# A causal depthwise convolution shared by VectorE and GpSimd, moved wholly to VectorE

## What is computed

```
z = rms_norm(x) @ w_in                     # columns: q | k | v | a (512) | b (512)
u = a * sigmoid(b)                         # gated linear unit (GLU), 512 channels
o = band_attention(rms_norm(q), rms_norm(k), v)
c[t] = b_dw + sum_{j=0..30} w_dw[j] * u_ext[t + j]    # per channel; 30 earlier rows in front
c = silu(layer_norm(c)) @ w_pw + b_pw
x = x + concat(rms_norm(o), rms_norm(c)) @ w_out
x = x + mixture_of_experts(x);  y = x + per_layer_gate(x)
```

## Time and profile before

| what | value |
|---|---|
| median of the three runs | 1662.56 us (1661.34 to 1664.23) |
| span of the profiled execution | 1662.2 us |
| TensorE busy | 1306.2 us, 79% |
| VectorE busy | 1166.7 us, 70% |
| GpSimd busy | 925.6 us, 56% |
| ScalarE busy | 694.7 us, 42% |
| mean granted TensorE clock | 0.907 of full speed |

### The profile page before, as it was taken

The page is one execution under the profiler, slowest core; times in us unless marked ns, Lnnn a source line. Parts: engine busy times, 40 slices in busy tenths (PEclk is TensorE's granted clock), DMA queues, the critical chain, the costliest instruction groups (busy, mean ns, idle before and its releaser), DMA issues.

```text
span 1662.2 us, 18411 instructions
## 1 busy us (share of the span) xinstructions
PE 1306.2 (79%) x5969; PEld 1043.3 (63%) x5969; DVE 1166.7 (70%) x1171; ACT 694.7 (42%) x833; POOL 925.6 (56%) x829
## 2 busy tenths in 40 slices
PE   1777678887755699906888888888888888886998
PEld 0666567675633588805776666766767666744776
DVE  2279969788878422294887998888888789844442
ACT  2322223333323322212665666666666666622121
POOL 1367739999951300043777777777777777730000
PEclk9998889798766799956999999999999999997999
DMA  5311010000010332122898888889999999963320
GB/s 181 109 51 31 12 57 14 24 10 4 28 51 25 127 127 76 38 102 69 291 312 320 301 307 299 303 306 311 326 317 327 318 321 326 330 219 127 123 81 32
DMA packets 122318, 279.76 MB, mean 168 GB/s; under 512 B 17537, under 2 KB 20033, under 8 KB 122269
## 3 DMA queue, kind: packets, MB, share of 16 engines
q1 hardware_dynamic: 112477, 261.28, 45.4%
q0 software_dynamic: 9792, 17.85, 2.9%
HBM read 269.85 MB, written 27.12 MB: 179 GB/s over the span
## 4 chain that ended last, share of the span: by engine, by line
PE 34%; issue 11%; DVE 8%; ACT 2%; DMA 1%; SPq 0%; DVEq 0%; POOL 0%; POOLq 0%; ACTq 0%
PE ps L407 10%; PE ps L408 10%; PE ps L409 10%; DVE ahl L388 2%; PE ps L1615 2%; DVE mem L1538 1%; PE ps L1966 1%; ACT hhl L1075 1%; PE ps L1928 1%; DMA mem<-y_rows 1%; DVE whl L388 1%; PE ps L1862 1%; PE ps L1938 0%; DVE hhl L388 0%; DMA mem<-in_g_ple 0%
## 5 line engine op out<-in xcount | busy, mean ns | idle before, releaser
L388 DVE TENSOR_TENSOR whl<-mem,whl 128x1280 fp32r<-128x1280 f32 (+1 forms) x205 | 506.8, 2503 | 27.1 <-ACT whl L1052 25.7
L388 POOL TENSOR_TENSOR whl<-mem,whl 128x768 fp32r<-128x768 f32 (+1 forms) x213 | 467.7, 2223 | 103.1 <-ACT whl L385 62.1
L407 PE MATMUL ps<-whl,ahl 128*128 128x512 f32 x1124 | 452.9, 403 | 73.5 <-DVE ahl L388 71.4
L1052 ACT ACTIVATE whl<-mem 128x2048 fp32r<-128x2048 f32 x196 | 375.9, 1919 | 178.5 <-PE ps L409 178.5
L408 PE MATMUL ps<-whl,ahl 128*128 128x512 f32 x1124 | 444.6, 396 | 0.0
L409 PE MATMUL ps<-whl,ahl 128*128 128x512 f32 x1124 | 442.8, 394 | 0.0
L407 PEld LDWEIGHTS ps<-whl,ahl 128*128 128x128 f32 x1124 | 221.5, 197 | 128.6 <-issue 71.9
L409 PEld LDWEIGHTS ps<-whl,ahl 128*128 128x128 f32 x1124 | 219.9, 196 | 45.4
L408 PEld LDWEIGHTS ps<-whl,ahl 128*128 128x128 f32 x1124 | 220.5, 196 | 42.6 <-issue 0.2
L459 DVE SCALAR_TENSOR_TENSOR mem<-mem 128x256 f32<-128x256 f32 (+1 forms) x270 | 199.5, 808 | 0.0
L668 POOL TENSOR_SCALAR mem<-mem 128x1 f32<-128x1 f32 (+1 forms) x54 | 21.5, 397 | 318.8 <-ACT mem L875 286.3
(11 more groups left out here) (234 smaller groups left out, 1415.6 us busy)
## 6 DMA issues: line engine op xcount, KB each, us to landing
mem<-in_w_e_up SPq DMA_DIRECT2D x66, 1024.0 KB, 7.5
mem<-in_w_e_down SPq DMA_DIRECT2D x66, 1024.0 KB, 6.8
mem<-in_w_e_gate SPq DMA_DIRECT2D x66, 1024.0 KB, 5.6
mem<-in_x_prompt SPq DMA_DIRECT2D x24, 512.0 KB, 3.4
mem<-y_rows SPq DMA_DIRECT2D x16, 512.0 KB, 5.6
mem<-in_w_in SPq DMA_DIRECT2D x4, 1024.0 KB, 8.7
mem<-in_w_out SPq DMA_DIRECT2D x4, 1024.0 KB, 4.9
h_rows<-mem SPq DMA_DIRECT2D x8, 512.0 KB, 2.6
```

The lines of the kernel that those rows point to most:

```text
L388: return which.tensor_tensor(out, full, hi.bitcast(F32), ALU.subtract)
L407: nc.tensor.matmul(out, act_hi, whl[:, 0, w_at], start=first, stop=False)
L1052: nc.scalar.activation(whl[:, 0, slot * CH:(slot + 1) * CH], raw[c], ACT.Copy).then_inc(s_mhi, 1)
```

## The change

The convolution is done by VectorE alone. It has three passes, each over all four channel groups: tiles 0 to 3 (512 columns), tiles 4 to 7 (512 columns), and the sample (64 columns). That makes 372 instructions, 248 of 512 columns and 124 of 64. The first pass can't begin before four tiles of `uT` are there. The table of the GLU stage now has none after tiles 0 to 3, 18 after each of tiles 4 to 7 and 20 after tile 8. Each attention step has 18 convolution instructions before `biased(t, 0)` and 14 before `qk_sums`, and what is left at t = 9 is nothing. GpSimd's taps are gone, with the semaphore `s_convs` and its waits on the engines SP, ScalarE and TensorE.

```diff
-        CONV_PARTS = ((0, 2, KC - 1), (2, 2, KC - 1), (4, 4, KC - 1))
-        CONV_OPS = sum(channels for _, _, channels in CONV_PARTS) * TAPS
-        CONV_FIRST = 2 * (KC - 1) * TAPS
+        CONV_PARTS = ((0, 4), (4, 4), (TS, 1))
+        CONV_OPS = len(CONV_PARTS) * KC * TAPS
+        CONV_FIRST = KC * TAPS
...
-            for t0, nt, channels in CONV_PARTS:
-                w, base = nt * P, t0 * P
+            for t0, nt in CONV_PARTS:
                 for j in range(TAPS):
-                    for c in range(channels):
-                        src = uT[:, c, base + j:base + j + w].rearrange("p (t n) -> p t n", n=P)
-                        acc = R[:, t0:t0 + nt, C + c * P:C + (c + 1) * P]
+                    for c in range(KC):
+                        if t0 < TS:
+                            src = uT[:, c, t0 * P + j:(t0 + nt) * P + j].rearrange("p (t n) -> p t n", n=P)
+                            acc = R[:, t0:t0 + nt, C + c * P:C + (c + 1) * P]
+                        else:
+                            src = uT[:, c, U_SAMPLE + j:U_SAMPLE + j + SAMPLE]
+                            acc = R[:, TS, C + c * P:C + c * P + SAMPLE]
...
-                            eng.wait_ge(s_conv, n - channels + 1)
+                            eng.wait_ge(s_conv, n - KC + 1)
...
-            def sample_tap(j):
...
-            def channel_tap(j, pair, where):
...
-            def conv_steps(first, last, where):
...
-                if t >= 5:
-                    conv_steps(POOL_EARLY * (t - 5), POOL_EARLY * (t - 4), early)
-            conv_steps(4 * POOL_EARLY, POOL_BEFORE, early)
...
-                conv_steps(POOL_BEFORE + POOL_PER_TILE * t, POOL_BEFORE + POOL_PER_TILE * (t + 1), late)
-            pool.sem_inc(s_convs, 1)
...
-            CONVS_BY_TILE = (0, 0, 26, 26, 26, 26, 26, 24, 18)
+            CONVS_BY_TILE = (0, 0, 0, 0, 18, 18, 18, 18, 20)
...
-                convs(6)
+                convs(18 if t < 9 else 0)
                 if t < NT:
                     biased(t, 0)
                 if t >= 1:
                     attention_out(t - 1)
-                convs(4)
+                convs(14)
```

More of the change, by code:

```diff
@@ L253, in build_step @@
         s_o = sem("attention_normed")
-        s_convs = sem("sample_conv_done")
         s_ones = sem("ones_made")
@@ L431, in build_step @@
         LOADS = NH + NKV + 2 + 1 + NG + 2
-        CONV_PARTS = ((0, 2, KC - 1), (2, 2, KC - 1), (4, 4, KC - 1))
-        CONV_OPS = sum(channels for _, _, channels in CONV_PARTS) * TAPS
-        CONV_FIRST = 2 * (KC - 1) * TAPS
-        POOL_STEPS = 5 * TAPS
-        POOL_FIRST = 2 * TAPS
+        CONV_PARTS = ((0, 4), (4, 4), (TS, 1))
+        CONV_OPS = len(CONV_PARTS) * KC * TAPS
+        CONV_FIRST = KC * TAPS
         TAPS_AT = KC * HALO + NKV * P
@@ L580, in _ @@
             sp.wait_ge(s_conv, CONV_OPS)
-            sp.wait_ge(s_convs, 2)
             for c in (2, 3):
@@ L683, in pool_chunk @@
                 mixer_lo(pool, nc.gpsimd, s_wlp, j, lo_cut(j), chunk_size(j))
-            POOL_EARLY, POOL_BEFORE, POOL_PER_TILE = 6, 36, 14
-            acc = R[:, TS, C:2 * C].rearrange("p (c n) -> p c n", c=KC)[:, :, 0:SAMPLE]
-            early, late = qT[:, C:C + 2 * P], u2[:, C // 2:C]
-            def sample_tap(j):
[L692 to L701, removed]
@@ L994, in _ @@
             act.wait_ge(s_kv, 16 * 6)
-            act.wait_ge(s_convs, 2)
             act.wait_ge(s_oe, NT)
@@ L1733, in channel_sums @@
                     pe.wait_ge(s_conv, CONV_FIRST)
-                    pe.wait_ge(s_convs, 1)
                     pe.wait_ge(s_xl, 4 * NT)
@@ L1777, in _ @@
             pe.wait_ge(s_conv, CONV_OPS)
-            pe.wait_ge(s_convs, 2)
             channel_sums(1)
```

## The result

The changed kernel takes 1667.95 us (median of 20 runs, 1665.88 to 1671.84), the kernel before 1662.46 us beside it (20 runs, 1657.92 to 1668.78). The ratio is 1.0035 with a 95% interval of 1.0026 to 1.0045: 5.5 us slower, just beyond what a measurement can tell from no change. 8 us were forecast. The profiled execution of the changed kernel has a span of 1665.1 us, 2.9 us above the 1662.2 of the profiled one before, so the two profiles show a part of the 5.5 us only.

What follows compares the result with a forecast made beforehand. VectorE and GpSimd were taken to share the attention stage's bound and slow each other. The terms -14.4 + 45.0 - 11.6 - 9.5 - 1.5 = +8.0 us, on the median of 1662.56, gave 1670.6 us, range 1658.5 to 1678.

Steps and rivals of the forecast that it cites:

- Price of an instruction: VectorE's convolution instructions without GpSimd's taps: 0.66 us for 512 columns, 0.19 for 64, in all 187 us.
- first taps: First instructions of each convolution, TENSOR_SCALARs priced as the others; 1.5 us off for the eight wide ones, estimated 0 to 3.
- The rival of 0.60 us: A wide VectorE instruction costs 0.60 us, not 0.66: 14.9 us less, sum -6.9, time 1655.7; chance 0.11.
- GLU stage: From the start to `qk_sums(0)`: it starts at 201.8 us instead of 216.1, 14.4 us gained.
- The second wait: GLU stage, after tile 5: VectorE waits 2.4 us because its stream holds GpSimd's `rstd`, as after tile 4.
- the last weight part's rival: GLU stage: GpSimd's fourth weight part waits for tile 8's stream, `qk_sums` starts at 206.5, 4.7 us later; chance 0.12.
- Tiles 0 to 4: Attention stage: steps of tiles 1 to 3 grow from 29.4 to 36.9 us, in all 45.0 us lost.
- Tiles 5 to 8: Attention stage: steps of 23.7 us each, between VectorE's list of 21.9 and tile 8's 25.0 before; 11.6 us gained.
- The rival in which TensorE keeps its clock: Tiles 5 to 8 take 22.5 us a step and the last step gains 12: sum +0.6, time 1663.2; chance 0.17.
- Last step: End of the attention stage, without its 17 convolution instructions: 9.5 us gained, between 8.2 and 12.
- GpSimd isn't held: GLU stage: `rstd` slips into VectorE's streams, two waits of 2.4 us go, sum +3.2, time 1665.8; chance 0.10.
- The sentence that the convolution is shorter as a whole, and that it is where it lies that counts: Convolution moves from steps two engines share into five where VectorE has it all; tiles 5 to 8, with room, get narrow ones.

Runs made afterwards that it cites:

- the even spread: The changed kernel with only the counts of convolution instructions in each attention step altered, 22 to 19 wide ones at t = 0 to 7, then the narrow ones: 1644.65 us.
- the kernel with the filled GLU stage: The even spread with 12 convolution instructions after tile 3 and 15 after each of tiles 4 to 7, in place of none and 18: 1637.37 us.
- the fastest one: The kernel with the filled GLU stage, with four convolution instructions issued between the two halves of x_lo in attention steps 0 to 7: 1620.50 us.

## Why the prediction was right

The direction, the time (5.5 us slower, 8 forecast) and the mechanism came out; point by point:

- **Price of an instruction.** 0.66 us was right for 512 columns. Narrow ones are 3.61 us for 18, so 0.20, against 0.19. Four first taps take 1.83 us from start to start (117.88 to 119.71), 0.46 each: 0.20 less than the others, 1.6 us for eight, where 1.5 was estimated. The rival of 0.60 us fell at once.
- **GLU stage**, forecast -14.4, and -15.2 with its half of the first taps; measured 201.68 - 216.13 = -14.45. That it is so near is in part luck. `ev` of tiles 5 to 8 came at 132.65, 147.98, 162.91 and 181.17, against 133.5, 149.5, 164.5 and 185.0. The second wait was GpSimd's product and not `rstd`, and cost 1.5 us and not 2.4. The four weight parts took 4.62 us and not 6.8. GpSimd had a part of its own to do beside them, as before, but it didn't get between them: that part lasted from 176.64 to 182.4, 5.75 us, past the end of VectorE's four. In turn the stream of tile 8 took 16.97 us and not 13.2: GpSimd's last three parts lie beside its start, to 188.5. So a part of the same contention was paid one tile later, and two misses of 3.8 us cancel. What the last weight part's rival feared, a start of `qk_sums` at 206, did not happen: no part was held to the end of that stream.
- **Tiles 0 to 4**, forecast +45.0, and +44.2 with the other half of the first taps; measured (391.22 - 211.67) - 135.1 = +44.4. The step at 319.06 was 36.96 us against 36.9.
- **Tiles 5 to 8**, forecast -11.6, measured 90.5 from 391.22 to 481.72 (0.67 us after the start of the norm at 481.05, as 467.71 was of before), so -16.0. Here is the term that was mis-sized. I took 23.7 us for each, between VectorE's list and tile 8 of before. The steps were 23.9, 23.9, 19.3 and 23.4: a mean of 23.7 without tile 7, whose step lacks the `x_lo` exchange and makes all of the 4.4 us. The trace of before shows that step 6 us shorter than the one ahead of it, and I had not looked. That VectorE's narrow instructions don't set these steps is shown: without them they stay. The rival in which TensorE keeps its clock had the better number, 22.5 us for a step against a mean of 22.6, but by luck: three of the four steps took over the 23 us at which it decides, and the clock was 0.93 to 0.98 in tiles 5 to 7 (0.86 to 0.90 before), but 0.50 in tile 8, as before.
- **Last step**, forecast -9.5, measured 12.2 against 20.7: -8.5. That is near the lower bound of 8.2: the end follows TensorE's last product with v by 3.25 us (493.91 - 490.66), where I had 3.4. The chain that I had made faster by a full clock ran at about the clock of before (0.81 against 0.77). From the end of VectorE's last `biased` to the end of that product it did take 9.5 us and not 10.7, but 1.0 of this lies ahead of 481.72 and so counts in the term above. The rival's 12 us for this step fell.
- Sum of the measured: -14.45 + 44.4 - 16.0 - 8.5 = +5.5 us at the end of the attention stage. That the medians differ by just as much is in part luck too, as the two profiled spans differ by 2.9.
- **GpSimd isn't held** was priced at -4.8 us, two waits of 2.4. It came true for one `rstd` of the two (0.44 us after tile 5), and the product behind it was held instead. Where GpSimd was let in on purpose, the waits went and the time did not: VectorE then stood for about as long. So the price of that rival was wrong, and not only its chance.
- **The sentence that the convolution is shorter as a whole, and that it is where it lies that counts,** is what the even spread showed: the same instructions gave 1644.65.

## What to carry to other kernels

Moving work off a slow engine onto the engine it disturbs ends the disturbance, but here it paid only once the work was spread over the steps by what each step had free. So fill each step's idle time of the receiving engine first, and see which engine sets a step before and after. Take the price of an instruction from a stretch in which its neighbour is silent, and look for the gaps inside a step, such as the wait between two halves of an exchange, since work put there costs least. Before one price is taken for several steps, look in the trace of before for a step that differs, above all the last ones. Compare an edit that changes data only up to the first branch that depends on data.

## What the hardware showed

- In the changed kernel a stream of VectorE instructions with two inputs from SBUF, issued without a gap, held off a one-column GpSimd instruction to the stream's end, 8.69 us, and a product likewise, 8.54, though each instruction of the stream lasts only 0.75. With one instruction of VectorE that reads nothing in every third place they took 0.74 and 2.58 us. The section "Who interferes with whom" on the page SBUF — State Buffer of the Trainium skill calls the shared port an exclusive lock that the first to issue has "for the whole instruction" (it says so of VectorE's two-port modes); by that a wait of one instruction would be expected, and the measured waits are those of a stream. One reading is that the next instruction of the stream takes the port again before GpSimd can; no run shows this. It is not always so. The one-column instruction took 0.44 us in the changed kernel's next stream, and 0.23 in two streams of the kernel with the filled GLU stage. GpSimd's weight parts ran beside the stream of tile 8, whose twenty instructions took 16.97 us. What decides between the two is open.
- GpSimd instructions that only write cost VectorE's stream nothing: beside fifty of them in a step its instructions stayed 0.66 us apart, and beside sixteen products that read two inputs they were 1.03 apart. This agrees with the same section of the Trainium skill, which says that the second input of VectorE comes through the read interface shared with GpSimd.
- TensorE's granted clock was higher in the attention stage where TensorE had more to do. The same stretch of the windows view, first of the changed kernel, then of the fastest one:

```profile
205.00:360.00 155.00, 107.59 (x520) 90.73 (x521) 135.54 (x214) 40.56 (x118) 10.89 (x14) 0.71 0.05 18
```

```profile
205.00:360.00 155.00, 125.25 (x726) 107.33 (x725) 145.86 (x233) 58.74 (x170) 16.71 (x22) 0.87 0.06 18
```

With 520 matmuls in 155 us the mean clock was 0.71, with 726 it was 0.87, and 40% more matmuls took only 16% more busy time. So the idle share of TensorE in the steps of 37 us overstates what the faster steps had to find: a part of the added products was paid by the clock. What sets the clock was not tried.
